# Second attention: VectorE scales the probabilities of step t-1 at the head of step t, and splits weights at the odd steps

## The reference, cut to what matters

```
# windowed                                   # neighbourhood
s = einsum(q, k) * dh**-0.5, masked          s = einsum(q_r, k_g) * scale + bias
m = maximum(max(s), sink)                    p = softmax(s)
e = exp(s - m)                               y = einsum(p, v_g)
p = e / (sum(e) + exp(sink - m))
y = einsum(p, v)
```

## Time and profile before

| | |
|---|---|
| median of 3 runs | 1801.7 us (1801.67 to 1803.37) |
| the profiled execution | 1805.36 us, its span 1803.6 us |
| busy over the span | PE 1721.3 us (95%), DVE 818.3 (45%), ACT 618.0 (34%), POOL 149.4 (8%) |
| mean granted TensorE clock | 0.98 of full speed (2.4 GHz) |
| chain that ended last | PE 86%, DVE 6%, ACT 3%, DMA 2%, issue 2% |
| second attention | 1105.1 to 1290.7 us of the span |

### The profile page before, as it was taken

One profiled execution on the slowest core, in us unless ns is written; L12 is line 12 of the kernel. 1 busy time (PEld: TensorE's weight loads), 2 busy tenths in 40 slices (PEclk: granted clock), 3 DMA queues, 4 the chain that ended last, 5 costly groups with the idle time before them and its releaser, 6 DMA issues.

```text
span 1803.6 us, 22674 instructions
## 1 busy us (share of the span) xinstructions
PE 1721.3 (95%) x7999; PEld 1374.7 (76%) x7999; DVE 818.3 (45%) x1250; ACT 618.0 (34%) x1063; POOL 149.4 (8%) x152
## 2 busy tenths in 40 slices
PE   5999698999999999999999998999899999999997
PEld 3767476888888878888888885666688888888886
DVE  4688635443333334444434325554455544444222
ACT  4365433232222332322222222544443423223222
POOL 0041111000001131000010040002000200000000
PEclk8999899999999999999999998998999999999999
DMA  8543113443333335333333263111232333333331
GB/s 336 194 131 110 47 47 94 131 133 97 97 108 96 90 89 136 102 93 93 101 115 96 83 150 75 48 48 56 68 96 85 90 102 95 93 98 107 103 96 63
DMA packets 296461, 184.54 MB, mean 102 GB/s; under 512 B 14923, under 2 KB 285767, under 8 KB 295367
## 3 DMA queue, kind: packets, MB, share of 16 engines
q1 hardware_dynamic: 290784, 169.89, 31.7%
q0 software_dynamic: 3968, 12.70, 2.9%
q10 hardware_dynamic: 1656, 1.25, 0.2%
HBM read 180.67 MB, written 6.36 MB: 104 GB/s over the span
## 4 chain that ended last, share of the span: by engine, by line
PE 86%; DVE 6%; ACT 3%; DMA 2%; issue 2%; SPq 0%; DVEq 0%; ACTq 0%
PE psum L539 27%; PE psum L541 27%; PE psum L540 27%; DMA ada_w<-in_w_ada 1%; PE psum L884 1%; DVE w_lo L1486 1%; PE psum L911 1%; PE psum L927 1%; DVE p L1567 1%; ACT w_hi L1091 1%; DMA w_raw<-in_w_in 1%; DVE p L1528 1%; ACT p L1156 1%; PE psum L684 1%; DVE acc L1479 0%
## 5 line engine op out<-in xcount | busy, mean ns | idle before, releaser
L539 PE MATMUL psum<-h_hi,w_hi 128*128 128x512 f32 x1480 | 590.0, 399 | 13.2 <-DVE w_lo L1486 6.7
L540 PE MATMUL psum<-h_lo,w_hi 128*128 128x512 f32 x1480 | 580.6, 392 | 0.0
L541 PE MATMUL psum<-h_hi,w_lo 128*128 128x512 f32 x1480 | 580.6, 392 | 0.0
L1486 DVE TENSOR_TENSOR w_lo<-w_raw,w_hi 128x1024 fp32r<-128x1024 f32 (+1 forms) x258 | 349.5, 1355 | 383.6 <-ACT w_hi L1091 380.5
L539 PEld LDWEIGHTS psum<-h_hi,w_hi 128*128 128x128 f32 x1480 | 280.6, 190 | 97.0 <-issue 29.4
L1091 ACT ACTIVATE w_hi<-w_raw 128x1024 fp32r<-128x1024 f32 (+1 forms) x258 | 286.6, 1111 | 157.4 <-PE psum L541 139.5
L541 PEld LDWEIGHTS psum<-h_hi,w_lo 128*128 128x128 f32 x1480 | 280.2, 189 | 60.0
L540 PEld LDWEIGHTS psum<-h_lo,w_hi 128*128 128x128 f32 x1480 | 280.8, 190 | 57.1 <-issue 0.7
L541 PE MATMUL psum<-hid_hi,w_lo 128*128 128x512 f32 x528 | 209.8, 397 | 0.0
L539 PE MATMUL psum<-hid_hi,w_hi 128*128 128x512 f32 x528 | 208.3, 395 | 0.0
L540 PE MATMUL psum<-hid_lo,w_hi 128*128 128x512 f32 x528 | 207.7, 393 | 0.0
(11 more groups left out here) (240 smaller groups left out, 1405.7 us busy)
## 6 DMA issues: line engine op xcount, KB each, us to landing
w_raw<-in_w_in SPq DMA_DIRECT2D x50, 512.0 KB, 3.9
w_raw<-in_w_gate_up SPq DMA_DIRECT2D x44, 512.0 KB, 3.8
w_raw<-in_ffn_w_gate SPq DMA_DIRECT2D x44, 512.0 KB, 3.8
w_raw<-in_ffn_w_up SPq DMA_DIRECT2D x44, 512.0 KB, 3.8
w_raw<-in_ffn_w_down SPq DMA_DIRECT2D x32, 704.0 KB, 4.5
sq<-in_w_ada SPq DMA_DIRECT2D x24, 512.0 KB, 4.6
w_raw<-in_w_down SPq DMA_DIRECT2D x16, 704.0 KB, 4.6
ada_w<-in_w_ada SPq DMA_DIRECT2D x8, 1024.0 KB, 17.7
```

Of the source, the lines that this page charges most:

```text
L539: pe.matmul(o, a_hi, b_hi, start=start, stop=False)
L540: pe.matmul(o, a_hi, b_lo, start=False, stop=False)
L541: return pe.matmul(o, a_lo, b_hi, start=False, stop=stop)
L1486: dve.tensor_tensor(w_lo[:, s % 2, 0:n], w_raw[:, s % 2, 0:n], w_hi[:, s % 2, 0:n].bitcast(F32), ALU.subtract).then_inc(w_ready, 1)
```

## The change

VectorE's part (3), the scaling of unit t-1, moves to the head of step t, ahead of (1) and (2). Part (4), split_low, moves from the even steps to the odd ones: the slab S_MIX2 + t // 2 + 1 is the same for t and t+1, so each split comes one step later, after that step's eviction and minima. No other engine's program is changed, and no instruction is added or removed.

```diff
             for t in range(UN2 + 3):
+                u = t - 1
+                if 0 <= u < UN2:
+                    windowed, w, st = unit2(u)[0], width2(u), stat2[:, u % 2, :]
+                    dve.wait_ge(expd2, exps2(u))
+                    if windowed:
+                        dve.tensor_tensor(st[:, 2:4], st[:, 2:4], st[:, 4:6], ALU.add).then_inc(summed2, 1)
+                        dve.wait_ge(summed2, u + 1)
+                    dve.reciprocal(st[:, 6:8], st[:, 2:4]).then_inc(recip2, 1)
+                    dve.wait_ge(recip2, u + 1)
+                    for j in range(2):
+                        dve.tensor_scalar(p2[:, u % 2, j, 0:w], p2[:, u % 2, j, 0:w], st[:, 6 + j:7 + j], None, ALU.mult)\
+                           .then_inc(combined2, 1)
                 if t >= 2 and t % 2 == 0 and t <= UN2:
                     j = t // 2 - 1
                     b = wait_filled(dve, ("slab", S_MIX2 + j))
...
                         dve.tensor_tensor(st[:, 8:10], st[:, 0:2], sink[:, c:c + 5:4], ALU.add).then_inc(scored2, 1)
-                u = t - 1
-                if 0 <= u < UN2:
...
-                if t < UN2 and t % 2 == 0:
+                if t < UN2 and t % 2 == 1:
                     split_low(S_MIX2 + t // 2 + 1)
```

## The result

| | before | changed |
|---|---|---|
| median, 20 runs each | 1802.5 us (1797.9 to 1806.6) | 1810.7 us (1805.1 to 1817.8) |
| ratio | | 1.0045, 95% interval 1.0033 to 1.0058 |
| profiled execution, span | 1805.4, 1803.6 | 1805.05, 1803.3 |

A forecast was written before the change was run, and what follows sets the result against it. The prediction took TensorE, busy for 95% of the span, as the bound; +4.5 us in stalls and +4.2 in clock made +8.7, and against the median 1801.7 a forecast of 1810.4 us, range 1802 to 1817.

The forecast's parts named there:

- Bank 7's hand-back: TensorE's matmuls at even t wait for the slab eviction, now behind the scaling; 2.9 us in each windowed group.
- Start: Start of the second attention: TensorE begins t = 2's matmuls at 1120.29 instead of 1121.53, -1.2 us.
- t = 3: First group: the split no longer stands before the scaling, so TensorE's wait at t = 3 goes, -1.4 us.
- Windowed groups: Three groups such as t = 6 to 8: TensorE starts the next slab 1.10 us later each, +3.3 together.
- Near group without GpSimd: t = 26 to 28, no minima or add: TensorE starts at 1265.74 instead of 1264.91, +0.8 us.
- Near groups with GpSimd: t = 19 and 23: GpSimd's building of near slows the split and the scalings, +1.9 and +1.1 us.
- the rival of 1815.8: Near groups: port lock held for GpSimd's whole build, +2.3 and +3.1 on the forecast; chance 0.05.
- Clock: New stalls bring 2.5 further falls of TensorE's granted clock at 1.7 us each, +4.2 us.
- What would show it: Signs: L927's wait under 5 us, L539's over 18, stage clock 0.93 or lower, split beside near over 2 us twice.
- The rival that no further fall of the clock comes: Stalls as laid out but no further clock falls: +4.5, 1806.2 us; chance 0.17.
- The faster rival: At TensorE's first matmul of even t, bank 7 doesn't decide: -11.7, 1790.0 us; chance 0.12.

The follow-up runs named there:

- e1: Changed kernel with the slab eviction put ahead of the scaling again, split still at odd steps: 1798.8 us, ratio 0.9978 to before.
- e5: Kernel before with only the scaling moved, behind the slab eviction and ahead of the eviction with minima; split at even steps: 1794.7 us.
- e7: Changed kernel with only the low part of the heads' output one step later, scaling still ahead of the slab eviction: 1788.8 us.
- e4: Changed kernel with unused matmuls added on TensorE before the slab's matmuls where it stalls: 1801.4 us, mean clock 0.9845.
- e8: Changed kernel with GpSimd's building of near for pairs 2 and 3 one step later: 1807.0 us in a single run.

## Why the prediction was right, and where it was not

The forecast was 1810.4 us and 8.7 slower; measured were 1810.7 and 8.2. Its steps:

- **Bank 7's hand-back, the mechanism.** Right: the wait under that name, 2.92 us against 2.9; e1 and e5 cut it by order, to 1.79 and 0.66, e7 by head start, to 0.55.
- **Start, -1.2.** Right: -1.37 less the -0.21 of the stage. **t = 3, -1.4**: -0.94 in the table. The wait went; 0.42 of it came back at the low clock, at which the twelve matmuls of t = 2 took 5.01 us instead of 4.59, and 0.2 at t = 4, where the eviction's start was taken as early enough. With that clock taken out it is -1.36.
- **Windowed groups, +1.10 each.** Right: +1.26, +1.17, +0.96 in the table of starts (the last is +1.19 with the low clock of t = 12 taken out, 4.45 us of matmuls there and 4.22 here).
- **Near group without GpSimd, +0.8.** Right: +0.9. (The table has -1.41 from t = 24 to 28; the matmuls of t = 24, at a low clock in the trace before, took 5.13 us there and 2.81 here, 2.3 us that have nothing to do with the order.)
- **Near groups with GpSimd, +1.9 and +1.1.** The mis-sized term: +0.6 and -0.2 (of the 1.92 from t = 16 to 20, 1.3 is a low clock before t = 18; the second is +0.6 too without the 0.8 of clock that the prediction takes off). The price of the split beside the building was taken from a split that began beside GpSimd's additions, 2.34 us. Here the split begins ahead of the building. VectorE's and GpSimd's timelines, and the durations of the building's six instructions (ns, least, median and longest):

```profile
1219.88 1.22 DVE L1486 TENSOR_TENSOR w_lo<-w_raw,w_hi 128x1024 fp32r<-128x1024 f32 x1
...
1221.21 1.35 DVE L1800 TENSOR_SCALAR p<-p,stat 128x256 f32<-128x256 f32 x2
```

```profile
1220.10 5.09 POOL L2013 TENSOR_TENSOR near<-near_mask,rel 128x256 f32<-128x256 f32 x6 [147.13 <-DVE stat L1826]
```

```profile
L2013 POOL TENSOR_TENSOR near<-near_mask,rel x6: 709/746/1576, 1220.1 to 1224.5; 128x256 f32<-128x256 f32 x6
```

The split began 0.22 us before the building and took its usual 1.22; the building took 5.09 instead of 4.25, nearly all of it in one instruction, 1.58 us where the median is 0.75. The scalings behind the split paid, 1.35 for two instead of 0.62. At t = 24 it is the same (1.22, 5.11, 1.34). The 0.22 could have been read before: the instruction after the evictions began at 1217.42 in VectorE's timeline and the building at 1217.64:

```profile
1217.42 0.16 DVE L1829 RECIPROCAL stat<-stat 128x2 f32<-128x2 f32 x1
```

The prediction's quotation from the Trainium skill, Trainium Architecture — The Big Picture, "What this means for kernel authors", that the contention of the two engines is an exclusive lock, agrees with this trace in that one of the two engines waits, 0.84 us of the split's last 1.00. It isn't held for the building's six instructions: the two scalings were done inside it. So the rival of 1815.8 falls.

- **Clock, +4.2.** About right: 5.4 by the line over the runs, some 4.4 by the two traces' waits. The count of falls was a guess at a mean: in the one trace the clock fell in or after the stalls at t = 2, 12, 16 and 20 and not at 8, 24 and 28. Of its five stalls of 2.8 to 2.9 us three were followed by the low clock, and of the five of 1.6 to 2.0 us at t = 7, 11, 15, 19 and 23 in the trace before three too. That trace has five falls in the stage, the changed one four. Where the further falls come in the other runs stays open.
- **What would show it.** The waits came as named, L927 at 4.3 us and L539 at 20.0. Two signs did not: no split beside `near` took over 2 us, and the granted clock of the stage is 0.95 in the profiled execution, the shortest, not 0.93 or lower.

In the prediction's own terms these steps add up to about +2.4 in stalls, and by the line over the runs to +3.2, instead of +4.5; nearly all that is missing lies in the groups with GpSimd. The clock came out 1.2 above. So two misses cancel in part, and the closeness of the total is partly luck. The rival that no further fall of the clock comes is refuted by the mean clocks, 0.9778 against 0.9811, and by e4. The faster rival failed at its place, bank 7: TensorE does wait there. Its time of 1790.0 is not reached even with the slab's eviction put first again (e1, 1798.8), where that eviction stands behind the split.

## What to carry to other kernels

Before moving a block up in an engine's queue, list every semaphore that the blocks it passes raise, and set the new chain's length beside the slack that the last waiter has: here 0.57 us (the slab's eviction ended at 1154.32, TensorE began at 1154.89) against a chain through another engine. The name of today's longest wait says what to shorten, not what will be next. When an order can't be changed, look for work without a near reader, as L1841 here, and push that back.

## What the runs showed of the hardware

- Of VectorE and GpSimd, with both at work on SBUF, the instruction under way kept its pace and one of the other engine waited for its end. A split (two inputs from SBUF) begun 0.22 us ahead of GpSimd's building took 1.22 us and one of the building's instructions 1.58 instead of 0.75, the whole building 5.09; a split begun behind GpSimd's additions took 2.34. Scalings (one input from SBUF) pay too: two took 1.35 to 1.62 beside the building, 0.62 alone; in e8, moved to the scaling of unit 20, 1.43, with 4.27 for the building.
- With the granted clock the same program's span moves by 13 us, from 1803.3 at 0.981 to 1816.0 at 0.973. A single profile of each kernel would have called the change nothing (1805.05 against 1805.4).
